# Seven edits around the expert stage, the opening of the second block, its memory keys and its layer norm

## The reference, cut to what matters

```
# first block
x  = x + merged @ w_out
h2 = rmsnorm(x, norm2_g)
x  = x + hierarchical_moe(h2, ...)      # 32 experts in 4 groups, 2 per token
# second block
xn   = rms_norm(x, norm_mix)
proj = xn @ w_in          # sparse attention q, k, v, 24 gate logits, conv, memory q, merge gates
kc   = rms_norm(gelu(blocks @ cmp_w1) @ cmp_w2)     # compressed keys
u    = silu(layer_norm(depthwise_conv31(a * sigmoid(ag)), g, b))
km   = rms_norm(heads((rms_norm(mem, norm_mem) @ w_mem_kv)[:, :512]))
h    = x + (g0 * nsa @ w_nsa_out + g1 * u @ w_conv_out + g2 * memory_attention @ w_mem_out) @ w_out
out  = h + (silu(hn @ w_gate) * (hn @ w_up)) @ w_down
```

## Time and profile before

| | us |
|---|---|
| median of 3 runs | 1888.69 (1885.57 to 1894.19) |
| profiled execution, its own time | 1894.05 |
| its span, first to last instruction | 1892.4 |
| PE busy | 1829.7 (97%) |
| granted TensorE clock, mean | 0.978 |
| DVE, ACT, POOL busy | 839.0, 587.9, 768.3 |

### The profile page before, as it was taken

The page is one execution under the profiler, slowest core; times in us unless marked ns, Lnnn a source line. Parts: engine busy times, 40 slices in busy tenths (PEclk is TensorE's granted clock), DMA queues, the critical chain, the costliest instruction groups (busy, mean ns, idle before and its releaser), DMA issues.

```text
span 1892.4 us, 23509 instructions
## 1 busy us (share of the span) xinstructions
PE 1829.7 (97%) x8839; PEld 1362.6 (72%) x8839; DVE 839.0 (44%) x1263; ACT 587.9 (31%) x1082; POOL 768.3 (41%) x629
## 2 busy tenths in 40 slices
PE   9999999999998999998999799999999999999999
PEld 6887777776887444443878576777778878888887
DVE  4122665544533233232433667998438452202221
ACT  3323344452332201101332335555334222212221
POOL 4454333342530000000332357888815545444452
PEclk9999999999998999999789899999999999999999
DMA  6322222223434989998323232222253322322321
GB/s 225 101 79 89 89 73 84 84 98 119 128 117 174 364 324 396 354 373 346 100 90 122 89 100 84 73 68 74 78 195 113 121 79 100 100 94 96 99 91 45
DMA packets 81895, 266.36 MB, mean 141 GB/s; under 512 B 8320, under 2 KB 9344, under 8 KB 81792
## 3 DMA queue, kind: packets, MB, share of 16 engines
q1 hardware_dynamic: 61152, 224.02, 33.9%
q10 hardware_dynamic: 18336, 32.51, 4.7%
q0 software_dynamic: 2304, 8.39, 1.3%
HBM read 248.11 MB, written 16.78 MB: 140 GB/s over the span
## 4 chain that ended last, share of the span: by engine, by line
PE 88%; DVE 7%; DMA 2%; ACT 1%; ACTq 1%; issue 1%; POOL 0%; SPq 0%; POOLq 0%; DVEq 0%
PE psum L560 85%; DMA more<-stream 2%; PE psum L1260 1%; PE psum L914 1%; ACTq L1828 1%; DVE area L1938 1%; PE psum L685 1%; DVE area L2461 1%; DVE area L1997 1%; DVE root L1922 1%; DVE area_r L1891 1%; ACT area L1407 0%; ACT root L1407 0%; DVE yt_lo L2245 0%; DVE area L1902 0%
## 5 line engine op out<-in xcount | busy, mean ns | idle before, releaser
L560 PE MATMUL psum<-area_r,ring_hi 128*128 128x512 f32 (+1 forms) x3168 | 999.4, 397 | 7.7 <-DVE area_r L1891 2.4
L458 POOL TENSOR_TENSOR ring_lo<-ring,ring_hi 128x512 fp32r<-128x512 f32 x436 | 588.3, 1372 | 874.4 <-ACT ring_hi L1407 870.1
L560 PEld LDWEIGHTS psum<-area_r,ring_hi 128*128 128x128 f32 x3168 | 592.7, 190 | 147.9 <-issue 25.6
L560 PE MATMUL psum<-area_r,ring_lo 128*128 128x512 f32 (+1 forms) x1584 | 618.6, 391 | 0.0
L1407 ACT ACTIVATE ring_hi<-ring 128x1024 fp32r<-128x1024 f32 x218 | 229.7, 1057 | 574.7 <-PE psum L560 543.4
L560 PEld LDWEIGHTS psum<-area_r,ring_lo 128*128 128x128 f32 x1584 | 300.5, 190 | 62.8
L1407 ACT ACTIVATE area<-psum 128x512 f32<-128x512 f32 (+3 forms) x256 | 124.6, 513 | 285.2 <-PE psum L560 94.7
L1922 DVE RECIPROCAL root<-root 128x512 f32<-128x512 f32 (+1 forms) x30 | 94.2, 3139 | 122.8 <-ACT root L1407 122.8
L560 PE MATMUL psum<-area 128*64 128x128 f32 (+6 forms) x832 | 112.3, 346 | 5.7 <-ACT area L1407 3.7
L560 PE MATMUL psum<-ring,area 128*64 128x512 f32 (+1 forms) x416 | 107.8, 609 | 1.0 <-DMA ring<-stream 0.6
L560 PE MATMUL psum<-more,area 128*64 128x512 f32 x384 | 92.2, 601 | 9.3 <-DVE area L2240 6.7
(11 more groups left out here) (217 smaller groups left out, 1661.9 us busy)
## 6 DMA issues: line engine op xcount, KB each, us to landing
ring<-stream SPq DMA_DIRECT2D x324, 512.0 KB, 3.5
more<-stream SPq DMA_DIRECT2D x48, 1024.0 KB, 9.3
area<-gates ACTq DMA_DIRECT2D x40, 256.0 KB, 5.6
gates<-root ACTq DMA_DIRECT2D x24, 256.0 KB, 2.0
gates<-area ACTq DMA_DIRECT2D x16, 256.0 KB, 2.2
area<-xT SPq DMA_DIRECT2D x8, 256.0 KB, 4.4
area<-xT ACTq DMA_DIRECT2D x8, 256.0 KB, 3.7
tokens<-area ACTq DMA_DIRECT2D x2, 1024.0 KB, 4.2
```

The source lines that it names most:

```text
L458: ins = nc.gpsimd.tensor_tensor(ring_lo[:, c % RS, n], ring[:, c % R, n], ring_hi[:, c % RS, n].bitcast(F32), ALU.subtract)
L560: return nc.tensor.matmul(out, lhsT, rhs, start=first, stop=last)
```

## The change

It reorders and joins work in seven places; the matrices computed are the same.

1. POOL's last `low` of the gate loop goes behind the split of the last tile.
2. In every group `turn(g, 3)` goes ahead of `unit(g, 15)`, and DVE's `turned(g, 3)` ahead of `low(g, 2)`.
3. The last group's last pair writes to banks 0 and 7 and doesn't wait for the pair before; its two parts are made in halves; the last 8 scatters use six banks and begin with the pair before it. Chunks of the next block are split inside the expert stage, for which `selT` and `more0` change places.
4. For the norm of the second block POOL adds three and DVE two pairs of squares, and PE sums 3 tiles instead of 8.
5. `opened`: vsw and the first kv tile advance together, k by k; the gate logits go between the tiles of the convolution.
6. ACT no longer waits for the memory's norm before q2; the norm's split is done inside q2's entries by ACT (`mem_high`) and DVE (`mem_low`); q2 and km are one chain of 12 entries, vm its tail; `gate2` waits for vm only from its first chunk on; DVE applies 30 taps ahead of the compressed keys' root instead of 22 ahead and 8 between entries.
7. The convolution's sums go inside the memory attention (`conv_sum`); the sums of squares become 16 matmuls with one column and root and reciprocal 128x4, spread by 4 matmuls; both `wide` calls go; the 24 gate reads go from ACT's queue to SP's, behind the load of merge chunk 8.

```diff
@@ sync
-            segment(CMP1 + R, NCHUNK, w_lo, R - 1 + MOE1 - MOE0 + CMP1 - CMP0)
+            MERGE = C0["merge2"] + 9
+            segment(CMP1 + R, MERGE, w_lo, R - 1 + MOE1 - MOE0 + CMP1 - CMP0)
+            sp.wait_ge(weights_used, C0["gate2"] + 3 * KD)
+            for j in range(2):
+                sp.wait_ge(S(f"gate_kept{j}"), 16 * 5 * KD // 2)
+            gates2(0, (0, 1))
+            sp.wait_ge(S("mo"), 16)
+            sp.wait_ge(S("conv_out"), 2 * TAPS)
+            sp.wait_ge(S("conv_pool"), 2 * TAPS)
+            gates2(0, (2,))
+            for p in range(1, 4):
+                gates2(p, (0, 1, 2))
+            segment(MERGE, NCHUNK, w_lo, R - 1 + MOE1 - MOE0 + CMP1 - CMP0)
@@ gpsimd
-                low(split_no(c) + 1, c)
+                if n < 2 * KD - 1:
+                    low(split_no(c) + 1, c)
...
+            low(split_no(C0["merge1"] + RS - 1) + 1, C0["merge1"] + RS - 1)
@@ gpsimd
-            split(MOE1, CMP0)
+            pool.wait_ge(weights_used, MOE1 - 4)
+            low(split_no(MOE1) + 1, MOE1)
+            low(split_no(MOE1 + 1) + 1, MOE1 + 1)
+            for n, (a, b) in enumerate(((0, 1), (2, 3), (0, 2))):
...
+                nc.gpsimd.tensor_tensor(tile(Q2 + a), tile(Q2 + a), tile(Q2 + b), ALU.add).then_inc(S("consts2"), 1)
+            pool.wait_ge(S("sp_x"), KD * 2 * GROUPS)
+            low(split_no(MOE1 + 2) + 1, MOE1 + 2)
+            low(split_no(MOE1 + 3) + 1, MOE1 + 3)
@@ tensor
+                    turn(g, PAIRS - 1)
                     unit(g, 15)
-                    turn(g, PAIRS - 1)
                     second(g, PAIRS - 1)
+                pe.wait_ge(S("sp_yl"), PAIRS * g + PAIRS - 1)
+                for m in range(4):
...
+                    last_scatter(PAIRS - 2, m)
                 for m in range(KD):
-                    scatter(GROUPS - 1, 1, m)
+                    if m % 4 == 0:
+                        pe.wait_ge(S("sp_yl"), PAIRS * GROUPS + m // 4)
...
+                    last_scatter(PAIRS - 1, m).then_inc(S("sp_s"), 1)
+                nx_sums()
@@ tensor
+            def opened(c):
+                for k in range(KD):
...
+                    pe.wait_ge(S("normout"), KD * NB["nx"] + k + 1)
+                    for t in range(NT):
...
+                        mm(out, hi, whi, k == 0 and t % 2 == 0, False)
+                        mm(out, hi, wlo, False, False)
+                        ins = mm(out, lo, whi, False, k == KD - 1 and t % 2 == 1)
...
+                    ins = mm3(psum[:, 0, :], parts(c, P * k, P * k + P), (tr(HH + k), tr(HL + k)), k == 0, k == KD - 1)
@@ tensor
-            normed("q2", q2_entries(), prior=cmp_sums)
-            pe.wait_ge(S("normout"), KD * NB["nm"] + 8)
-            normed("km", km_entries(), prior=lambda j: pe.wait_ge(S("hdout"), HB["q2"] + 5 + j))
+            normed("q2", q2_entries() + km_entries(), prior=cmp_sums, ready=mem_ready,
+                   tail=lambda x: vm_steps((1, 2, 3) if x else (0,)))
@@ tensor
             branch(0, 0)
-            branch(0, 1)
-            wide(16, 5)
             for c in range(CONVT):
                 pe.wait_ge(S("ln_sq"), c + 1)
-                ins = mm(psum[:, 7, :], ones[:], tile(SCR2 + c), c == 0, c == CONVT - 1)
+                for t in range(NT):
+                    ins = mm(psum[:, 7, t:t + 1], tile(SCR2 + c)[:, P * t:P * t + P], ones[:, 0:1], c == 0 and t == 0,
+                             c == CONVT - 1 and t == NT - 1)
+            ins.then_inc(S("ln_sum"), 1)
+            branch(0, 1)
...
-            wide(20, 5)
@@ scalar
-            act.wait_ge(S("normout"), KD * NB["nm"] + 8)
-            normed("q2", q2_entries())
-            act.wait_ge(S("hdout"), HB["q2"] + 8)
-            normed("km", km_entries())
+            normed("q2", q2_entries() + km_entries(), between=mem_high)
@@ vector
-            conv_taps(0, 22)
+            conv_taps(0, 30)
             dve.wait_ge(S("cmp_root"), 1)
...
-            normed("q2", q2_entries(), lambda j, to: tile(to), between=lambda j: conv_taps(22 + j, 23 + j))
-            normed("km", km_entries(), lambda j, to: km_tiles[:, j, :])
+            normed("q2", q2_entries() + km_entries(), lambda j, to: tile(to) if j < 8 else km_tiles[:, j - 8, :],
+                   between=mem_low)
```

More of the change, by code:

```diff
@@ L640, in normed @@
                         prior(j)
+                    if ready is not None:
+                        ready(j)
+                    if j == 0 and opened is not None:
+                        opened(c)
+                        continue
                     wait_chunk(c)
@@ L1037, in second @@
                         pe.wait_ge(S("sp_selT"), PAIRS)
-                    if g or p:
+                    if (g or p) and not last:
                         pe.wait_ge(S("sp_yl"), g * PAIRS + p)
@@ L1671, in gathered @@
                     silu(g, 3)
-                    high(g, 2)
-                    high(g, 3)
+                    if more:
+                        high_pair(g, 2)
+                        high_pair(g, 3)
+                g = GROUPS - 1
+                preload(ACT.Sqrt, 5)
+                act.wait_ge(S("sp_t"), PAIRS * GROUPS)
+                high(MOE1)
+                high(MOE1 + 1)
+                high_pair(g, 2)
+                act.wait_ge(S("sp_s"), KD * 2 * g)
+                high(MOE1 + 2)
+                high(MOE1 + 3)
+                act.wait_ge(weights_used, MOE1)
+                for x in range(2):
+                    A(yt_hi[:, PAIRS - 1, 512 * x:512 * x + 512], psum[:, LAST2[x], :], ACT.Copy).then_inc(S("sp_yh"), 1)
             def dense():
@@ L1683, in dense @@
                             A(root[:, f, :], psum[:, 4 * (n % 2) + 2 * f, :], ACT.Silu).then_inc(S("fb_silu"), 1)
+                preload(ACT.Sqrt, 5)
+                for c in range(RS):
+                    high(MOE1 + c)
             act.wait_ge(S("flag_ok"), 1)
@@ L1692, in _ @@
             used[0] = MOE1
-            def loads2():
-                for c in range(RS):
-                    high(MOE1 + c)
-            norm("nx", lambda k: tile(X + k), lambda k: tile(Q2 + k), then=loads2,
+            norm("nx", lambda k: tile(X + k), lambda k: tile(Q2 + k),
                  ready=lambda k: act.wait_ge(S("sp_x"), KD * (2 * GROUPS - 1) + k + 1))
@@ L1702, in _ @@
                 act.dma_start(x_dram[k], tile(X + k)).then_inc(S("stored"), 16)
[L1703 to L1707 removed]
+            follow(C0["vsw"] + 1)
+            act.wait_ge(weights_used, C0["vsw"] + 2)
+            for j in range(2):
+                A(tile(VSW + j), psum[:, 2 + j, :], ACT.Copy).then_inc(S("vsw_out"), 1)
             for k in range(KD):
```

248 lines of the change are left out of this document (160 added, 88 removed).

## The result

The changed kernel took 1840.63 us (median of 4 runs, 1839.02 to 1845.29), beside it the kernel before 1887.13 (4 runs, 1883.42 to 1894.19): ratio 0.9753, interval 0.9719 to 0.9788, so 2.5% faster. 1837 was predicted. The profiled execution has a span of 1839.2 us against 1892.4: 53.2 less, where the sum said 52.2. The medians differ by less, 46.5: the profiled execution of the kernel before (1894.05) is one of its slower ones (35 executions stand on record, 1883.3 to 1896.4, their median 1889.5), that of the changed kernel (1840.79) lies at its median.

The account below looks back on a forecast made before the run. PE, busy 97% of the span, was taken to bound the kernel by its work, waits and slow clock. Savings of 1.7 + 4.6 + 10.5 + 8.7 + 16.2 + 10.5 = 52.2 gave 1836.5 from the 1888.69 median, predicted 1837, range 1830 to 1845.

Parts of the forecast that it names:

- Edit 1: Gate loop before merge1: POOL's split runs earlier, so PE's 2.24 us wait goes; -1.7, bounds -2.2 and 0.
- Edit 2: Expert group ends: scatter matmuls cover DVE's copy, the 1.67 us waits go; -4.6, between -1.6 and -6.4 as loads may pace.
- Edits 3 and 4: End of expert stage: scatters fill the wait and three tiles are summed; -10.5, sums end at 908.2 for 918.7.
- Edit 5: Second block's opening, vsw to kv's second tile: no waits from tile to tile, 33.2 us for 41.9; -8.7.
- Edit 6: Memory keys, q2 to nsa: waits and slow clock gone, -23.2; POOL held up by DVE's taps, +7.0; together -16.2.
- Edit 7: Layer norm to first cv tile: 15.4 us of replaced work and waits becomes 4.9; -10.5, bounds -11.5 and -6.
- POOL gets the port between two taps: Rival ahead of q2: the POOL stall is absent, 7.0 us less, 1829.5; chance 0.20.
- The clock comes back less and loads pace: Rival: new short PE waits bring slow stretches, 10.4 us, and loads pace the expert groups, 3.0; 1850, chance 0.20.
- Half of edits 5 to 7 is lost: Rival: edits don't add up, a wait moves behind each; 17.7 us lost, 1854, chance 0.11.
- The slower rival: Rival in the joined q2 and km chain: each of 16 chunks costs 4.7 us more; 1874 to 1912, chance 0.02 for slower.
- the first rival: The rival in which POOL gets the port between two taps, 1829.5, chance 0.20; used for the low end, 1824.
- the second and fourth rival: Slower clock with loads pacing (1850, chance 0.20) and half of edits 5 to 7 lost (1854, 0.11); high end 1856.

Follow-up runs that it names:

- e9: The changed kernel with POOL's rest of the weights put back ahead of the last tile's split in the gate loop; 1843.5 us, ratio 0.9741.
- e2: The changed kernel, but DVE stops after 14 of its 30 taps until POOL has split q2's first two chunks; 1838.11 us, ratio 0.9732.
- e11: The changed kernel with the layer norm's 32 one-column matmuls spread between the k steps of the second branch tile; 1838.99 us, ratio 0.9718.
- e4: The changed kernel with each group's last turn put back after its last scatter unit, on PE and DVE; 1850.87 us, ratio 0.9793.
- e7: The changed kernel with the third pair's eight scatter matmuls after the wait for the last pair's rests, not before it; 1844.98 us, ratio 0.9762.
- e6: The changed kernel without adds of squares on POOL and DVE: PE sums all eight tiles, 64 one-column records for 24; 1851.34 us, ratio 0.9798.
- e10: The changed kernel with all vsw matmuls first, then kv's first tile, in place of both in each step; 1840.26 us, ratio 0.9731.
- e1: The changed kernel with the old tap order: 22 DVE taps ahead, 8 one by one between q2's entries; 1833.46 us, ratio 0.9708.
- e3: The changed kernel with 28 of DVE's 30 taps reading their second tile from PSUM, sum over taps left out; 1836.53 us, ratio 0.9715.
- e8: The changed kernel with the 24 gate-value loads issued by ACT ahead of the layer norm's squares, not by SP; 1856.58 us, ratio 0.9827.
- e12: The changed kernel with old tap order, 8 layer-norm sum records (three DVE adds) between k steps, two fillers for four before the second block's spread; 1829.83 us, ratio 0.9686.

## Why the prediction was right

Step by step; a stretch's number is from the table of marks.

- **Edit 1, -1.7: measured -1.8, by its undoing (e9) 1.8.** Right, in mechanism and size. Merge1 starts 2.5 earlier, but 0.6 of that stood ahead of the edited place (415.25 against 415.88). The prediction took 0.5 off the wait of 2.24 for POOL beside DVE's softmax; the trace has it as waits for L2093, 0.24 and 0.83 in place of 0.45, so 0.6.
- **Edit 2, -4.6: measured 2.2 + 4.4 = -6.6.** The mis-sized term. It stood between 1.6 and 6.4, with loads pacing three of the groups. They don't: all four waits of 1.67 went, 6.7 together, and those for `more` stayed (2.6 before, 2.5 after). The waits are the firmer number: from the stage's first transpose to the end of `second` the changed kernel takes 287.2, and e2, e9 and e11, with the same order in that stage, 285.3 to 285.6. A DMA share of 0.94 and 2.6 us of waits in the whole span were not enough ground for a discount. And the step had a side that the prediction did not see: e4 shows that edit 3 needs it, for 3.7 + 2.8 more.
- **Edits 3 and 4, -10.5: measured -10.6.** The sums end 12.7 after `second`, where 12.5 was written. Of the parts, e7 gives the filling 2.7 and e6 the three sums 4.3. The 24 records took 4.1, as said (896.75 to 900.84).
- **Edit 5, -8.7: measured -8.9.** No wait from tile to tile after the first; e10 shows that joining kv's tile to the steps is worth 2.8 of it. The slow clock at the start, put at 2, came ahead of the first vsw matmul instead (0.61 over 900.9 to 906.6, 1.00 from there to the compressed keys). In its place stand two waits for ACT, 1.7 together (0.7 in one before), and some 0.8 that no row names: that the total fits to 0.2 is in part luck.
- **Edit 6, -23.2 and +7.0 = -16.2: measured -14.2 up to nsa's start and -2.1 of slow clock behind it, -16.3.** In that, POOL: a wait of 4.19 (4.8 said) and 2.8 of slow clock (2.2 said), 7.0 together by e1 (7.0 said), with a POOL instruction of 10.79 (about 11 said). The gains by themselves are then 23.3. Both terms are right, and e3 shows the reason behind the second; that this one fits to the tenth is luck, since its two parts missed by 0.6 each way.
- **Edit 7, -10.5: measured -9.9.** The slow stretch that was left possible is there, 1359 to 1362.5, and costs about 1.7. The first cv tile comes 6.2 us after the second branch tile's end (1362.74), where about 7 was written. What the step left in the shade is where its gain comes from: it called ACT's 13.8 us of issue shed work. e8 shows that it is the condition of the edit. The 13.9 us of fillers and waits of before were the other side of those loads.

The rival "POOL gets the port between two taps" is out by the 10.79. "The clock comes back less and loads pace" is out by edit 2 and by the even clock in the opening. "Half of edits 5 to 7 is lost" is out by the marks. The slower rival, POOL held up in every chunk of q2 and km, is out too: behind the first chunk PE has no wait for POOL at all, and POOL's pairs take 2.5 to 2.8 us.

The sum came out better than its parts: the edits' stretches add to 54.1, 1.9 over the 52.2, most of it from edit 2; 0.6 stood ahead of edit 1, and the clock between 440 and 460 took 1.6 back. The profiled execution took 1840.79 where 1841.9 was said. The median is 3.6 above the predicted one because the 5.4 between profiled execution and median, taken over from the kernel before, was 0.2 here. Here too is some luck. All prices were read from one execution of the kernel before, which lies well above its median, so the sum of 52.2 fits the difference of two traces and is too large for a typical execution: the medians differ by 46.5, by 48.9 with all 35 executions of the kernel before. Which of the stretches held the excess, one trace can't show.

Two sums of the prediction don't follow from its own terms, and neither bears on the result. The low end, the first rival with edits 2 and 5 at their upper bounds, gives 1829.5 - 1.8 - 2.3 = 1825.4 and not 1824. The high end, the second and fourth rival together, gives 1836.5 + 13.4 + 17.7 = 1867.6 and not 1856.

## What to carry to other kernels

When DVE's work is moved in front of a point, ask what POOL has to deliver there: a train of two-operand instructions from SBUF can stop POOL until its end, and one operand from PSUM, or eight of its instructions moved behind the point, shortens the stop. A filler or a wait on the busiest engine may be the cover of something else, here of 12 us of DMA issue; take the two away together or not at all. Runs of one-column matmuls are cheaper made fewer, by adds on an idle engine, than spread out; and when runs scatter by several us, read small edits between marks in the trace, not from medians, with one mark ahead of the edited place: 0.6 of the 2.5 us of edit 1 stood there already.

## What the runs showed of the hardware

- POOL was held up by DVE's taps for 5.5, 6.0, 7.5 and 10.8 us, each time until 1.1 to 1.2 us after the last one, and 1.27 with one operand from PSUM (e3). In the other direction DVE's products of 256 columns take 0.76 each beside POOL (1.07 in e2) and 0.41 alone.
- Behind 32 records of one column, with PE busy without a gap, the clock fell to its lower level (1.2 GHz), with 512-column matmuls between them too: 0.74 over ten us in e11, 0.83 in the changed kernel. With 8 records (e12) it stayed at 1.00. The Trainium skill (TensorE: Matmul & The Clock Gate, "Part 1: The HAM clock gate") has the clock follow how busy PE is; the busy time in the profile is 10.00 of 10.00 in both of these rows and does not tell it.
- The clock also fell between 440 and 460, amid unbroken work, to 0.74 to 0.85 by the trace; and the wait at the start of the expert stage, 2.8 to 5.1 us (in e6 two of them, 7.6 together), for the gather or for nothing shown, changed from kernel to kernel. Neither was settled; together they move the first transpose of that stage by up to 3.6 us (598.91 to 602.53) with nothing edited ahead of it.
